# Late modulation sums on GpSimd in the window-attention stage: eight weight tiles scaled first and folded as a tree, with one 2 MB load per step in place of two halves

## The reference, cut to what matters

```python
D_MODEL, SEQ, CTX_LEN, WINDOW = 1024, 1024, 256, 128

def hybrid_layer(x, ctx, c, c_ctx, ..., w_ada, b_ada, ...):
    mod_x = (jax.nn.silu(c) @ w_ada + b_ada)[:, None, :]
    ...
    sh_a_x, sc_a_x, g_a_x, sh_f_x, sc_f_x, g_f_x = jnp.split(mod_x, 6, axis=-1)
    ...
    y_at_x = window_attention_latent(qx, kx, vx, kc, vc, attn_sink)
    x = x + g_a_x * merge_branches(y_dn_x, y_at_x, mg_x, w_branch_dn, w_branch_attn, w_out)
    x = x + g_f_x * conv_ffn(modulate(rms_norm(x, norm_ffn), sh_f_x, sc_f_x), ffn_up, ffn_conv, ffn_conv_b, ffn_down)
```

## Time and profile before

| | us |
|---|---|
| time before, median of 3 runs | 2522.56 (2516.53 to 2523.92) |
| time of the profiled execution | 2523.92 |
| span of the profiled execution | 2522.0 |
| window-attention stage, first scores to last gate product | about 232.2 to 422.7 in the span |
| late modulation loads in it | 16 of 1024 KB |

### The profile page before, as it was taken

One profiled execution on the slowest core, in us unless ns is written; L12 is line 12 of the kernel. 1 busy time (PEld: TensorE's weight loads), 2 busy tenths in 40 slices (PEclk: granted clock), 3 DMA queues, 4 the chain that ended last, 5 costly groups with the idle time before them and its releaser, 6 DMA issues. The chain is left out here.

```text
span 2522.0 us, 40583 instructions
## 1 busy us (share of the span) xinstructions
PE 2432.3 (96%) x16150; PEld 2055.9 (82%) x16150; DVE 1448.7 (57%) x2281; ACT 824.2 (33%) x1900; POOL 886.1 (35%) x664
## 2 busy tenths in 40 slices
PE   5999999999999999999999999999899999999999
PEld 3778998888788888888888877878688888887887
DVE  5994774223666666766666752357755555564332
ACT  4223664101445454554545552111211111111100
POOL 1543984323423233241323222336333333332121
PEclk9999999999999999999999999999999999999999
DMA  7421332222001010010101003324311111114442
GB/s 254 111 76 68 126 133 82 88 84 73 21 10 35 17 36 26 18 35 10 35 9 35 26 18 109 100 88 139 136 51 51 50 46 47 51 37 128 124 135 91
DMA packets 53801, 177.02 MB, mean 70 GB/s; under 512 B 5488, under 2 KB 15088, under 8 KB 51312
## 3 DMA queue, kind: packets, MB, share of 16 engines
q1 hardware_dynamic: 51312, 170.24, 21.0%
q10 hardware_dynamic: 2304, 4.20, 0.4%
HBM read 148.20 MB, written 20.97 MB: 67 GB/s over the span
## 5 line engine op out<-in xcount | busy, mean ns | idle before, releaser
L205 PE MATMUL late_ps<-h_hi,late_w_hi 128*128 128x512 f32 x784 | 306.8, 391 | 6.6 <-ACTq L127 3.9
L207 PE MATMUL late_ps<-h_hi,late_w_lo 128*128 128x512 f32 x784 | 306.4, 391 | 0.0
L206 PE MATMUL late_ps<-h_lo,late_w_hi 128*128 128x512 f32 x784 | 306.2, 391 | 0.0
L188 POOL CAST late_w_hi<-late_w_raw 128x1024 fp32r<-128x1024 f32 x76 | 80.4, 1058 | 505.7 <-issue 377.6
L1509 PE MATMUL late_ps<-h_hi,dn_w_hi 128*128 128x512 f32 (+1 forms) x640 | 246.7, 385 | 0.0
L1509 PE MATMUL late_ps<-h_hi,dn_w_lo 128*128 128x512 f32 (+1 forms) x640 | 245.9, 384 | 0.0
L1509 PE MATMUL late_ps<-h_lo,dn_w_hi 128*128 128x512 f32 (+1 forms) x640 | 244.7, 382 | 0.0
L195 POOL TENSOR_TENSOR late_w_lo<-late_w_raw,late_w_hi 128x1024 fp32r<-128x1024 f32 x76 | 205.3, 2702 | 6.1
L2626 DVE SCALAR_TENSOR_TENSOR ffn_u<-ffn_pad,vectors,ffn_u 128x1024 f32<-128x1024 f32 (+1 forms) x90 | 198.1, 2201 | 3.2
L205 PEld LDWEIGHTS late_ps<-h_hi,late_w_hi 128*128 128x128 f32 x784 | 148.0, 189 | 38.2 <-issue 7.5
L206 PEld LDWEIGHTS late_ps<-h_lo,late_w_hi 128*128 128x128 f32 x784 | 148.0, 189 | 31.2 <-issue 0.2
(11 more groups left out here) (398 smaller groups left out, 6309.7 us busy)
## 6 DMA issues: line engine op xcount, KB each, us to landing
late_w_raw<-in_w_up SPq DMA_DIRECT2D x44, 512.0 KB, 3.5
down_w_raw<-in_w_down SPq DMA_DIRECT2D x32, 704.0 KB, 4.3
late_w_ada<-in_w_ada SPq DMA_DIRECT2D x16, 1024.0 KB, 4.8
dn_w_raw<-in_w_dn SPq DMA_DIRECT2D x32, 512.0 KB, 3.7
w_ada<-in_w_ada SPq DMA_DIRECT2D x8, 1024.0 KB, 11.1
at_w_raw<-in_w_mg_at SPq DMA_DIRECT2D x16, 512.0 KB, 4.0
late_w_raw<-in_w_mg_dn SPq DMA_DIRECT2D x16, 512.0 KB, 3.6
late_w_raw<-in_w_out SPq DMA_DIRECT2D x16, 512.0 KB, 3.7
```

Of the source, the lines that this page charges most:

```text
L188: pool.tensor_copy(self.hi[j][:, :, :], self.raw[j][:, :, :]).then_inc(self.hi_made, 1)
L205: pe.matmul(out, self.hi[j][:, k, :], xh, start=(k == 0), stop=False)
L206: pe.matmul(out, self.hi[j][:, k, :], xl, start=False, stop=False)
L207: mm = pe.matmul(out, self.lo[j][:, k, :], xh, start=False, stop=(k == self.kt - 1))
```

## The change

The sum of one step is written out as a whole. GpSimd multiplies all eight slices in place, then folds the tile as a tree: slices 4..7 onto 0..3 (two additions of 1024 columns), slices 2..3 onto 0..1 (one of 1024 columns), slice 1 onto 0 into `ada_acc` (one of 512 columns). Low parts of the queries stand between them at fixed places, so that one step goes with 8 units and not 7. The two semaphores of the tile become one: a step waits for the whole 2 MB tile, and the next tile is loaded, in one transfer, after the last fold of the step. The two `split_tile` calls come after the last fold of steps 0 and 1. The units at which TensorE takes the columns (10+7n to 13+7n) stay the same.

```diff
-    HALF_K, SPLIT_AT = KT // 2, (10, 20)
...
-                def ada_sum(n, k):
-
-                    pool.wait_ge(ada_in[k // HALF_K], n * 16 + 16)
-                    acc, c, w = ada_acc[:, n % 2, :], core.silu_c[:, k, 0:1], w_ada[:, k, :]
-                    if k == 0:
-                        if n >= 2:
-                            pool.wait_ge(ada_used, n - 1)
-                        ins = pool.tensor_scalar(acc, w, c, 1.0, ALU.mult, ALU.mult)
-                    else:
-                        pool.tensor_scalar(w, w, c, 1.0, ALU.mult, ALU.mult).then_inc(ada_scaled, 1)
-                        pool.wait_ge(ada_scaled, n * (KT - 1) + k)
-                        pool.wait_ge(ada_summed, n * KT + k)
-                        ins = pool.tensor_tensor(acc, acc, w, ALU.add)
-                    ins.then_inc(ada_summed, 1)
-
-                done = 0
-                for u in range(AHEAD, UNITS):
-                    queries_low(u, 1)
-                    while done < min(ADA_STEPS * KT, (u - AHEAD + 1) * KT // STEP_UNITS):
-                        ada_sum(*divmod(done, KT))
-                        done += 1
-                    if u - AHEAD in SPLIT_AT:
-                        at_w.split_tile(pool, SPLIT_AT.index(u - AHEAD), 0, SPLIT_AT.index(u - AHEAD), freed=False)
+                FIRST = 3
+                queries_low(AHEAD, FIRST)
+                for n in range(ADA_STEPS):
+                    u = AHEAD + n * XCH
+                    pool.wait_ge(ada_in, n * 16 + 16)
+                    pool.sem_inc(turns, 1)
+                    for k in range(KT):
+                        ins = pool.tensor_scalar(w_ada[:, k, :], w_ada[:, k, :], core.silu_c[:, k, 0:1], 1.0, ALU.mult,
+                                                 ALU.mult)
+                        if k == KT // 2 and n:
+                            queries_low(u, 1)
+                    ins.then_inc(ada_scaled, 1)
+                    if n:
+                        queries_low(u + 1, 1)
+                    pool.wait_ge(ada_scaled, n + 1)
+                    if n >= 2:
+                        pool.wait_ge(ada_used, n - 1)
+                    pool.tensor_tensor(w_ada[:, 0:2, :], w_ada[:, 0:2, :], w_ada[:, 4:6, :], ALU.add)
+                    if n:
+                        queries_low(u + 2, 1)
+                    pool.tensor_tensor(w_ada[:, 2:4, :], w_ada[:, 2:4, :], w_ada[:, 6:8, :], ALU.add).then_inc(ada_folded, 1)
+                    queries_low(u + 3, 1)
+                    pool.wait_ge(ada_folded, n * 3 + 1)
+                    pool.tensor_tensor(w_ada[:, 0:2, :], w_ada[:, 0:2, :], w_ada[:, 2:4, :], ALU.add).then_inc(ada_folded, 1)
+                    queries_low(u + 4, 1)
+                    pool.wait_ge(ada_folded, n * 3 + 2)
+                    pool.tensor_tensor(ada_acc[:, n % 2:n % 2 + 1, :], w_ada[:, 0:1, :], w_ada[:, 1:2, :],
+                                       ALU.add).then_inc(ada_folded, 1)
+                    queries_low(u + 5, 1)
+                    if n < 2:
+                        at_w.split_tile(pool, n, 0, n, freed=False)
+                    queries_low(u + 6, 2)
...
-                            pe.wait_ge(ada_summed, (n + 1) * KT)
+                            pe.wait_ge(ada_folded, n * 3 + 3)
...
-                    for i in range(2):
-                        ks = slice(i * HALF_K, (i + 1) * HALF_K)
-                        if n:
-                            sp.wait_ge(ada_summed, (n - 1) * KT + (i + 1) * HALF_K)
-                        sp.dma_start(w_ada[:, ks, :], d["w_ada"][:, n + 2 * KT // SLOT_T, ks]).then_inc(ada_in[i], 16)
+                    if n:
+                        sp.wait_ge(ada_folded, n * 3)
+                    sp.dma_start(w_ada[:, :, :], d["w_ada"][:, n + 2 * KT // SLOT_T]).then_inc(ada_in, 16)
```

More of the change, by code:

```diff
@@ L774, in window_attention @@
         q_hi_made, q_lo_made = core.sem("q_hi_made"), core.sem("q_lo_made")
-        ada_in, mod_made = [core.sem(f"late_ada_in{i}") for i in range(2)], core.sem("late_mod_made")
+        ada_in, mod_made = core.sem("late_ada_in"), core.sem("late_mod_made")
         with ExitStack() as shared:
@@ L788, in window_attention @@
         pt_act, pt_dve, y_ready = Count(core, "pt_act"), Count(core, "pt_dve"), Count(core, "y_ready")
-        ada_scaled, ada_summed, ada_used = core.sem("late_ada_scaled"), core.sem("late_ada_summed"), core.sem("late_ada_used")
+        ada_scaled, ada_folded, ada_used = core.sem("late_ada_scaled"), core.sem("late_ada_folded"), core.sem("late_ada_used")
         y_stored = core.y_stored = [nc.alloc_semaphore(f"y_stored{j}") for j in range(2)]
```

## The result

| | before | changed |
|---|---|---|
| time, median of 5 runs, us | 2522.56 | 2537.48 (2535.06 to 2541.04) |
| ratio to before, 95% interval | | 1.0069 (1.005 to 1.0088) |
| time of the profiled execution, us | 2523.92 | 2534.82 |
| span of it, us | 2522.0 | 2532.9 |

The change costs 14.9 us by the medians; the prediction was 10.7, within a range that reached to 2540. So the time lies inside the range, but above the forecast's own band (+7.6 to +13.5, chance 0.60) and in that of the dear rival (+13.5 to +19, chance 0.17). On another chip the two were run side by side again (experiment 0): 2534.15 against 2520.51, ratio 1.0059 (1.0046 to 1.0072), 13.6 us. Two executions far outside, one of the kernel before at 7134 us beside experiments 1 to 4 and one of experiment 11 at 8538 us, count in no ratio.

The account below looks back on a forecast made before the run. TensorE's own work was taken as the bound, until an unhidden load and folds made a 23.03 us loop against its 22.16. Step 7's sums at 415.6 instead of 404.84 gave 2522.56 + 10.7 = 2533.3 us, range 2528 to 2540.

Parts of the forecast that it names:

- the dear rival: Everything on GpSimd is dearer, by longer folds, a load of 8.5 us or a lower TensorE clock: +13.5 to +19 us, chance 0.17.
- dearer folds: Part of the dear rival (0.17): at 2.70 us each, the 24 long folds on GpSimd add 8.9 us.
- What bounds the stage: TensorE's own work sets the stage, 22.16 us per head of 8 units; a saving on GpSimd is worth nothing as such.
- GpSimd's work: Sums of one step on GpSimd: 14.8 us before, 13.5 after; a fold of 1024 columns takes 2.33 us.
- The load: The 2 MB load takes 7.35 us from its issue to GpSimd's start, with nothing of it overlapping the folds.
- The loop: Steps 1 to 6: 15.65 us of GpSimd's work plus 0.03 + 7.35 give 23.03 us, where TensorE wants one per 22.16.
- My bound from above (8.5): Upper bound of the 2 MB load, 8.5 us, from the first pair of halves; would add 8 us over seven passes.
- Step 0: First step: load issued at 231.53, lands at 240.1, last fold ends at 254.7, step 1 starts at 262.1.
- Step 7: Last step: starts at 400.3, sums there at 415.6 against a column taken at 404.84 before, so 10.7 us delay.
- The clock: Within the dear rival (0.17): TensorE's stand of 3.1 us before step 7's column could lower its clock, costing 1.7 us.
- The early load: Rival: the 2 MB load lands sooner than 7.35 us, at 6.9 or 6.5; +4 to +7.5 us, chance 0.18.
- the low parts made ahead would hide the load: Rival "not slower": GpSimd's low parts, up to four units (11 us) ahead, hide the load; 2522 to 2523 us, chance 0.05.

Follow-up runs that it names:

- experiments 1 to 4: Changed kernel with halved load, tree kept: 2519.75 us; columns one unit later: 2533.45; kernel before with single load alone: 2561.18; changed kernel fetching half the load: 2519.97.
- experiment 11: Changed kernel with load in halves and, in step 0, low parts of units 7 and 8 earlier and the sixth before the split: 2519.93 us, ratio 0.9997.
- Experiment 2: Changed kernel with TensorE's columns one unit later (11+7n instead of 10+7n), nothing else: 2533.45 us, ratio 1.0051.
- experiment 3: Kernel before with one 2 MB load per step, issued after the last slice is summed, sums still slice by slice: 2561.18 us, ratio 1.0168.
- 0 and 5: 0: the changed kernel itself again, 2534.15 us; 5: changed kernel with the 2 MB as two 1 MB loads, both after the last fold, 2532.68 us.
- experiment 6: Changed kernel with the low part of unit 7 moved, in step 0 alone, between the multiplications: 2536.11 us, ratio 1.0062.

## Why the prediction was right, point by point

**Where it came out.** The mechanism was right: one chain of load, multiplications and folds, a little slower than TensorE's pace, that TensorE is held to. The forecast was 4 to 5 us too small, since its sum held neither long loads nor the clock (3.8 us together in this profile). The range was drawn wide enough for them, but for other reasons: a constant longer load, or dearer folds. That the time lies inside it is therefore in part luck.

**What bounds the stage.** Right. TensorE's own work did (no wait for GpSimd, twice the same 192.7 us), and relieving GpSimd of 6.2 us of busy time in the stage gained nothing.

**GpSimd's work.** Right. A fold of 1024 columns lets the next start after 2.34 us (2.33 taken); a step from its first multiplication to the end of its last fold is 15.7 (15.65).

**The load.** The value was right and the spread was missed. Alone it lands in 7.1 to 7.3 us, and GpSimd starts 259.20 - 251.89 = 7.31 after the issue (7.35 taken). The fit of the Trainium skill that was cited there ("DMA: Bandwidth & Descriptors", "Anatomy of one DMA") gives 6.8; the page states it for a DMA issued from GpSimd, and these are issued from SyncE, so it was not the right rule for this load, and the measurement decides. But loads 2 and 5 took 8.4 and 8.0. The loop was 23.02 to 23.15 us where the load was quick, as computed, and 24.34 and 23.88 where it wasn't: 1.3 + 0.85 = 2.2 us that the sum lacked. My bound from above (8.5) had them, but I gave it to a rival as a constant, not to two loads in seven (four in experiment 0).

**Step 0.** The last fold ended 251.86 - 228.41 = 23.45 us after the issue, 23.2 in the sum. Its waits are where they were placed: 1.39 at scores(7), 0.63 at 8 and 10 (somewhat over 1 forecast), 1.45 at scores(12) (1.4).

**Step 7 and the total at its column.** It came 186.95 us after the first issue, where before had 173.31: 13.6 us late and not 10.7. Long loads are 2.2 of the difference, step 0 0.25, steps 4 and 6 0.12 each, and step 7 itself 0.25 (from its issue to its sums 22.90 us, 22.65 in the sum). That the column stands at 415.36 in the span, close to the 415.6 that was named as a sign, is luck: this execution entered the stage 3.1 us earlier. TensorE stood there for 2.98 us (3.1 forecast). Experiment 2 shows that this last wait is a term of its own, made by columns that go by 7 units and steps that go by 8.

**The clock.** It stood among the rivals as an addition of 1.7 us. It happened: 21.07 - 19.40 = 1.67 us. The Trainium skill, "TensorE: Matmul & The Clock Gate", part 1, cited there for idleness halving the clock, agrees: the granted clock went to 0.50. Had I counted it, the sum would be 12.4.

**The rivals.** The early load is excluded (no load below 7.1 us). That the low parts made ahead would hide the load is excluded by TensorE's ten waits and by the time, and in experiment 3 the same reserve did not hide it either. Dearer folds are excluded by their 2.37 us. The time fell into that rival's band all the same, through its other half: long loads and the clock.

**What stays open.** Which thing makes some loads long, and whether the low clock at the stage's entry in four of the profiles is chance.

## What to carry to other kernels

Before a buffer's refill is made one large transfer, write down the loop that it closes: last read, transfer, first use, last read. If that loop is longer than the consumer's period, an engine with plenty of idle time becomes the bound, and its idle time in the profile is the symptom, not a reserve. A tree that frees half of its inputs early keeps the refill hidden if those halves are fetched first, and where a consumer's cadence (7 units) differs from the producer's (8), it is the last period that shows the slip.

## What the runs showed of the hardware that I had not expected

The same 2 MB load takes 7.1 to 7.4 us, or 7.6 to 8.7, the latter mostly in steps 2, 5 and 7. These are the queues (packets, MB, share of 16 engines) in 8 us from the issue of load 2 of the changed kernel, which took 8.4, and then of load 3, which took 7.1:

```profile
q1 hardware_dynamic: 144, 2.10, 68.8%
q8 instruction: 1, 0.02, 0.7%
```

```profile
q1 hardware_dynamic: 144, 2.10, 67.8%
```

The long one shares its time with one packet of instructions. In the seven profiles with such loads (49 of them, after step 0), 14 had an instruction packet in their first 6 us, and all took 7.6 to 8.6 us; 25 had none in 7 us, and 24 of these took 7.1 to 7.4; of 10 with a packet first in the seventh microsecond, four were long (7.7 to 8.7). In experiment 3, whose step 2 falls at another time and meets no packet, it took 7.4. That is a coincidence in time, seen often; no run moved the packets alone, so the cause is not shown.

The lower clock followed waits of TensorE of 1.94 to 1.97 us (twice in experiment 2, once each in 0 and 5) as well as of 3 us, but not those of 2.02 at scores(20) in the changed kernel, 2.02 at scores(44) in experiment 0 and 2.09 at scores(20) in experiment 6. So the same wait can cost 1.4 to 1.6 us more or nothing, and no run here shows what decides it.
